# A bitwise top-k search on VectorE: constants of the two small operations as immediates instead of operands read per row

## What is computed

```python
def indexer_scores(q_idx, w_idx, k_idx, valid):
    dots = jnp.einsum("bqhd,bld->bqhl", q_idx, k_idx, ...) * (IDX_DIM ** -0.5)
    s = jnp.einsum("bqh,bqhl->bql", w_idx * (N_IDX_HEADS ** -0.5), jax.nn.relu(dots))
    return jnp.where(valid, s, -jnp.inf)

scores = indexer_scores(qib, wb, k_idx, valid)
_, sel = lax.top_k(scores, n_sel)          # n_sel = 256
# ... softmax attention of 8 query heads over the keys and values at sel
```

## Time and profile before

| | us |
|---|---|
| median of 3 runs | 2703.07 |
| lowest and highest | 2699.61, 2709.8 |
| span of the profiled execution | 2691.5 |

### The profile page before, as it was taken

The page is one execution under the profiler, slowest core; times in us unless marked ns, Lnnn a source line. Parts: engine busy times, 40 slices in busy tenths (PEclk is TensorE's granted clock), DMA queues, the critical chain, the costliest instruction groups (busy, mean ns, idle before and its releaser), DMA issues.

```text
span 2691.5 us, 34212 instructions
## 1 busy us (share of the span) xinstructions
PE 2205.6 (82%) x12640; PEld 1731.7 (64%) x12640; DVE 1858.8 (69%) x4093; ACT 757.6 (28%) x1415; POOL 120.6 (4%) x174
## 2 busy tenths in 40 slices
PE   7999999999788888778788786868686858888755
PEld 4777777776666665656666565756574748668652
DVE  2444444343148888998988989898989988734670
ACT  1111011110133333433434333343443415332000
POOL 0000000000000000000000000000000000000013
PEclk9999999999678887989888886969798889987556
DMA  6111111111411001100100100000000000114000
GB/s 256 64 69 67 49 63 70 70 39 39 174 42 42 28 24 40 42 19 26 40 10 32 34 11 32 11 32 11 32 9 10 24 18 17 34 63 134 1 10 23
DMA packets 53609, 121.82 MB, mean 45 GB/s; under 512 B 12944, under 2 KB 25912, under 8 KB 52448
## 3 DMA queue, kind: packets, MB, share of 16 engines
q1 hardware_dynamic: 51296, 109.53, 11.6%
q0 software_dynamic: 2176, 10.49, 1.2%
HBM read 81.11 MB, written 38.90 MB: 45 GB/s over the span
## 4 chain that ended last, share of the span: by engine, by line
PE 45%; DVE 38%; issue 10%; ACT 3%; DMA 1%; POOL 1%; PEld 1%; SPq 1%; DVEq 0%; ACTq 0%; POOLq 0%; PEldq 0%
DVE sb_junk L917 13%; PE psum L568 12%; PE psum L601 9%; PE psum L1138 6%; DVE sb_sc L902 5%; PE psum L1130 4%; DVE sb_p L936 3%; PE psum L1149 3%; PE psum L1107 2%; DVE sb_g L953 2%; PE psum L1120 2%; DVE sb_c L959 2%; PE psum L616 1%; DVE sb_sc L1068 1%; PE psum L1581 1%
## 5 line engine op out<-in xcount | busy, mean ns | idle before, releaser
L917 DVE TENSOR_SCALAR_CACHE_REDUCE sb_junk<-sb_sc,sb_c 128x384 bf16<-128x384 f32 (+13 forms) x434 | 641.1, 1477 | 11.6 <-DVE sb_mix L1051 2.4
L568 PE MATMUL psum<-sb_w,sb_xt 128*128 128x512 f32 (+5 forms) x1088 | 324.8, 459 | 0.5 <-DVE sb_xt L382 0.5
L1120 PE MATMUL psum<-sb_ks,sb_qa 128*128 128x512 f32 (+3 forms) x640 | 194.4, 439 | 148.2 <-ACT sb_p L855 109.7
L1138 PE MATMUL psum<-sb_v,sb_ptb 128*128 128x64 f32 x2176 | 298.8, 281 | 6.3 <-ACT sb_ptb L821 5.0
L1138 PEld LDWEIGHTS psum<-sb_v,sb_ptb 128*128 128x128 f32 x2176 | 286.3, 203 | 16.3 <-ACT sb_ptb L821 15.2
L1130 PE MATMUL psum<-sb_con,sb_p 128*128 128x128 f32 x1280 | 233.9, 310 | 67.6 <-ACT sb_p L863 44.7
L821 ACT ACTIVATE sb_ptb<-psum 128x512 f32<-128x512 f32 (+3 forms) x352 | 188.3, 539 | 296.2 <-PE psum L1130 295.9
L1149 PE MATMUL psum<-sb_wo,sb_mix 128*128 128x512 f32 x512 | 258.6, 669 | 13.5 <-DVEq L1054 13.5
L568 PEld LDWEIGHTS psum<-sb_w,sb_xt 128*128 128x128 f32 (+1 forms) x1088 | 178.5, 185 | 134.6 <-issue 125.1
L1107 PEld LDWEIGHTS psum<-sb_qa,sb_w 128*128 128x128 f32 x2048 | 248.2, 194 | 19.7 <-DMA sb_w<-in_w_in 6.6
L1107 PE MATMUL psum<-sb_qa,sb_w 128*128 128x128 f32 x2048 | 253.1, 278 | 6.1 <-DMA sb_w<-in_w_in 4.5
(11 more groups left out here) (318 smaller groups left out, 2228.0 us busy)
## 6 DMA issues: line engine op xcount, KB each, us to landing
qt_s<-sb_qt SPq DMA_DIRECT2D x32, 512.0 KB, 2.7
sb_x<-in_x_prompt SPq DMA_DIRECT2D x16, 512.0 KB, 3.8
xt_s<-sb_xt SPq DMA_DIRECT2D x16, 512.0 KB, 2.6
sb_qa<-xt_s SPq DMA_DIRECT2D x16, 512.0 KB, 3.4
sb_qa<-qt_s SPq DMA_DIRECT2D x16, 512.0 KB, 3.4
sb_xres<-in_x_prompt SPq DMA_DIRECT2D x16, 512.0 KB, 4.9
out_y_prompt<-sb_y SPq DMA_DIRECT2D x16, 512.0 KB, 3.0
sb_qi<-qt_s SPq DMA_DIRECT2D x14, 512.0 KB, 5.8
```

The costliest lines, as they stand in the source:

```text
L568: mm = pe.matmul(out, m.xt[:, p, k, 0:n], m.w1[:, k, lo:hi], start=(k == 0), stop=(k == KD - 1))
L917: return dve.tensor_scalar(m.junk[:, 0:w], m.sc[:, i % 2, 0:w], m.c[:], 0.0, ALU.is_ge, ALU.add, accum_out=m.cnt[:])
L1120: mm = pe.matmul(m.score2(slot)[:, lo:lo + n], m.qa[:, h, :], m.ks[:, 2 * kv + x, c[0] + lo:c[0] + lo + n], start=(x == 0), stop=(x == 1))
L1138: mm = pe.matmul(o, m.ptb[:, g, x * P:(x + 1) * P], v, start=st, stop=sp)
```

## The change

The weight of the bit and the next bit become immediates of the instructions, computed when the program is built (`next_bit`), and the two parts of the table go. The operations, their order and their waits stay; so does the count `m.k`, which differs from row to row and is still an operand.

```diff
@@ CONST_PARTS
     ("causal", 128),
-    ("pow", 32),
-    ("bit", 32),
     ], [
@@ constants
-    put("pow", np.tile(2.0 ** (30 - np.arange(32, dtype=np.float32)), (P, 1)).astype(np.float32))
-    bit = np.array([1 << (29 - n) if n < 30 else 0 for n in range(32)], np.int32)
-    put("bit", np.tile(bit.view(np.float32), (P, 1)))
@@
+def next_bit(it):
+
+    return 1 << (BITS - 2 - it) if it < BITS - 1 else 0
@@ search
-        ch.inc(dve.tensor_scalar(m.g[:], m.cnt[:], m.k[:], m.part("pow")[:, it:it + 1], ALU.is_lt, ALU.mult))
+        ch.inc(dve.tensor_scalar(m.g[:], m.cnt[:], m.k[:], float(2 ** (30 - it)), ALU.is_lt, ALU.mult))
...
-        ch.inc(dve.scalar_tensor_tensor(out=m.c[:].bitcast(I32), in0=m.c[:].bitcast(I32), scalar=bits[:, it:it + 1],
+        ch.inc(dve.scalar_tensor_tensor(out=m.c[:].bitcast(I32), in0=m.c[:].bitcast(I32), scalar=next_bit(it),
                                         in1=m.g[:], op0=ALU.bitwise_or, op1=ALU.bitwise_xor))
@@ c_vector
-        ch.link(dve.tensor_scalar(m.gi[:], m.lt[:], m.part("pow")[:, it:it + 1], None, ALU.mult))
+        ch.link(dve.tensor_scalar(m.gi[:], m.lt[:], float(2 ** (30 - it)), None, ALU.mult))
         ch.link(dve.scalar_tensor_tensor(out=m.cc[:].bitcast(I32), in0=m.cc[:].bitcast(I32),
-                                         scalar=bits[:, it:it + 1], in1=m.gi[:], op0=ALU.bitwise_or,
+                                         scalar=next_bit(it), in1=m.gi[:], op0=ALU.bitwise_or,
                                          op1=ALU.bitwise_xor))
```

More of the change, by code:

```diff
@@ L883, in b_vector @@
     causal = m.part("causal")
-    bits = m.part("bit").bitcast(I32)
     ch.inc(dve.tensor_copy(m.bias[:, 0, 0:P], causal))
```

## The result

The changed kernel takes **2670.8 us** (median of 4 executions, 2667.36 to 2680.19) against 2702.03 of the kernel before beside it: ratio 0.9884, 95% interval 0.986 to 0.9908. That is inside the range of 2647 to 2680 and 10 us above the forecast of 2661. So the change brings some 30 us, not 42.

The account below looks back on a forecast made before the run. DVE was taken to bound late boundary stretches, PE early ones, both by turns the heads. (176 + 167) x 0.112 = 38.4, plus decode 3.8, gave 42.2 us; 2691.5 - 42.2 + 11.6 = 2661 us, range 2647 to 2680.

Parts of the forecast that it names:

- The price of an operand: Each search's two small DVE operations: one operand fewer saves 57 ns on the compare, 55 on the set-bit, 112 together.
- the wait on POOL: Small DVE operations: immediate forms would wait beside POOL's work, some 22 us, half the gain; with no-change rival, 2703, chance 0.04.
- An operand thus holds the engine some 60 ns there too, and I take 112 ns everywhere.: Where a mask or accumulation follows a small operation, the successor still starts earlier; every counted search saves 112 ns.
- the lower end that I had named: Where unrelated work such as a mask or accumulation follows a small operation, the saved operands gain nothing.
- The late boundary stretch: A late step's last gated mix to the next memory-score maximum, 79.80 us, DVE busy 78.63: should shrink by 1.8 us.
- operands cost nothing where other work stands between: Rival: about half of the counted searches, those with other work between, drop out, 19.6 us; time 2680, chance 0.08.
- The boundary stretches: From a step's last gated mix to the next memory-score maximum: 176 of 224 searches count, at 0.112 us each.
- The heads: From a step's memory-score maximum to its last gated mix: 167 searches count, at 0.112 us each.
- what would be wrong: Signs against the forecast: durations that stay or fall without earlier next starts, head stretches that don't move, a clock falling there.
- slower, by PE's clock: Rival: late heads at PE's lower clock, 3 us each, 28 heads, 84 us lost; net 42 slower, 2745, chance 0.03.
- The decode: Decode search, 31 serial rounds: two small operations save 66 and 57 ns, 3.8 us in all.
- So 11.6 lie around the span.: Whole kernel: median time 2703.07 less profiled span 2691.5 taken as 11.6 us outside the span, added to the forecast.

Follow-up runs that it names:

- The short sequences: Changed kernel with 64 DVE sequences (large, small, large operation; 16 kinds) added ahead of stage B, other engines waiting; 2749.07 us, only its timeline used.

## Why the prediction was right, and where it was not

**The price of an operand.** Right, a little low: 61 and 61 ns, where I had 57 and 55. The rows with one operand fewer in the same kind of operation were good measures. None of the 434 takes more than 216 and 161 ns, so the wait on POOL that a rival named isn't there. The rule of the Trainium skill (VectorE: DVE Perf Modes, the section on the TRN2 errata), with a fixed cost and the columns alone, would have given nothing; the measured 271 to 210 ns at one column speak against its use for operations with operands per row.

**"An operand thus holds the engine some 60 ns there too, and I take 112 ns everywhere."** This step failed. The short sequences show that it is true of DVE by itself. It is false in the kernel, as the accumulation has a second wait, whose bound of 0.187 us by chance equals that of two operands, 0.184: the 0.18 us of the earlier trace rows had two causes of equal size, and I saw one. Behind 185 small operations with an accumulation, and 56 with a mask, the lower end that I had named was the right one, nothing. The late boundary stretch shows the size: 1.8 us forecast, 0.8 measured, 2.1 once the waits are exchanged. The rival *operands cost nothing where other work stands between* named these places, without the wait that is their reason. It took 19.6 us from the 42.2 and so left 22.6, too little, since it dropped such rounds whole. Of the 223 rounds with other work between, 56 have only the maximum, and there both operations paid; in 37 the set-bit has nothing behind it and paid; in 56 more the maximum behind the set-bit gave 0.014 us.

**The boundary stretches.** Forecast 19.7 us, 18.7 of them from step 5 on. That all searches from there on count was right: DVE's starts give 10.4 us in steps 5 to 14 by the table of start-to-start times, and the stretches became 10.5 shorter, one by one (1.02 and 1.04 in steps 7 to 9, 0.72 and 0.73, 0.71, 0.71 in 11 to 13). So in these steps the miss is the price alone, and it is most of the 8 us that this term was too large, of 12 in the sum. The last stretch, where PE has nearly as much work as DVE, gave -0.07, 0.43 and 0.56 us in the three profiles, against 0.56 forecast. The first four I had at nothing or 0.3 us each; in the profiles of the changed kernel their lengths change by +0.7 to -1.3 us, in sum by -1.3, +0.1 and -1.3, and with exchanged waits they gain nothing; PE leads there.

**The heads.** Forecast 18.7 us; DVE's starts give 18.9, for more searches at a lower mean price. Where the clock was about the same, the stretches took it over whole: 1.77 of 1.75 in step 7 (0.93 to 0.91), 0.96 of 0.95 in step 9 (0.85 both), 1.05 in step 11, 1.04 in step 14. So at an unchanged clock I was too careful with the heads late in a stretch. Steps 6 and 8 gained 2.7 and 3.3 with a higher clock (0.86 to 0.93 in step 8). In steps 12 and 15 the clock fell, which I had named as what would be wrong, and they became 9.1 us longer. The rival *slower, by PE's clock* had the mechanism and not the size: it needed 14 heads, and the falls come and go from profile to profile, in kernels with the table and without it.

**The decode.** 3.8 forecast, 3.6 measured; 169 and 160 ns where I had 162 and 164.

**"So 11.6 lie around the span."** Wrong. I took the median of some executions and the span of another. All that lies around the span of one execution is 1.8 us (2667.36 and 2665.6 in the profile of after). The rest goes mostly with the clock: the profiled execution of before had 2691.5 us at a mean clock of 0.856, while 41 others had 2694.1 to 2711.1 (median 2703.1) at 0.844 to 0.856 (median 0.850). Over these 41, 0.01 of clock goes with 15 us of span (correlation -0.82; the expectation above had said 19), so 0.006 goes with some 9 us by this estimate. The pairing did little harm to the time, since the changed kernel pays for its usual clock too, but the heads of before that I read were better than usual, and a head stretch 3 us longer than one of those need be no loss of the change.

**The sum.** From DVE's starts it would be 10.4 in the boundary stretches, 18.9 in the heads and 3.6 in the decode, 32.9 us. Between the medians of the spans, 2703.1 and 2672.9, lie 30.2. The boundary stretches (11.7, 12.2 and 10.7 in three profiles, the early ones among them) and the decode are there in every profile; the heads with their clock are left with about 15, and how much of the missing 4 is clock can't be told from the runs. Nor is the 30 free of the clock: the 12 executions of the changed kernel have a median clock of 0.8535, the 41 of the kernel before 0.850, and at 15 us for 0.01 that would be 5 us, an estimate. The intervals exclude no change and slower. That the range held is no sign that the sum was right: a gain of 30 us instead of 42 lies in it because its upper end allowed for half the gain.

## What to carry to other kernels

A scalar that is the same for all rows and known when the program is built is worth about 60 ns as an immediate in a DVE operation on a handful of numbers, but only where nothing else holds the next start. Before a start-to-start time is booked to the operation ahead, look for a second wait of the successor that ends at the same moment; in this kernel the start came 0.06 us earlier when the wait that ends last was the one that travels with the instruction, though the gain in the whole time, some 4 us, isn't certain. And a span is to be set against the time of its own execution, at its own clock.

## What the hardware showed unexpectedly

The order of two waits ahead of one DVE operation matters: with the two exchanged the accumulation starts 0.06 us earlier, 185 times, with the same two waits. A DVE operation that doesn't depend on the small one ahead starts 0.07 us after it where that has immediates alone, 0.13 where it has one operand per row and 0.19 where it has two, while the small one's durations are 0.15, 0.21 and 0.27: each operand adds to the spacing what it adds to the duration. And one stretch with the same code, step 12's heads in the changed kernel with its waits in either order, took 65.9 to 72.2 us from profile to profile, at a mean clock from 0.86 to 0.76.
